# Six weight granules of the first projection multiplied in plain float32

## The reference, cut to what matters

```python
cond = silu(c)                                  # (1, 2048)
for layer in range(2):
    mod = cond @ ada_w[layer] + ada_b[layer]    # ada_w: 2048 x 6144 a layer
    shift, scale, gate = split(mod, 3)
    h = rms_norm(x, norm_w[layer]) * (1 + scale) + shift
    if layer == 0:                              # 16 heads of 128
        q, k, v, z = split(h @ w_in, 4)         # w_in: 2048 x 8192
        y = (attention(rope(norm(q)), rope(norm(k)), v) * silu(z)) @ w_out
    else:
        y = mlstm_branch(h, ...)                # w_in: 2048 x 16400, w_out: 4096 x 2048
    x = x + gate * y
```

## Time and profile before

| | us |
|---|---|
| median of 3 runs | 1509.64 |
| the profiled execution | 1510.05 |
| its span | 1508.2 |
| PE busy in the span | 1446.7 (96%) |
| DVE busy | 1105.2 (73%) |
| ACT busy | 744.6 (49%) |
| 16 DMA engines, hardware queue | 72.4% |
| HBM over the span | 239 GB/s |

### The profile page before, as it was taken

One profiled execution on the slowest core, in us unless ns is written; L12 is line 12 of the kernel. 1 busy time (PEld: TensorE's weight loads), 2 busy tenths in 40 slices (PEclk: granted clock), 3 DMA queues, 4 the chain that ended last, 5 costly groups with the idle time before them and its releaser, 6 DMA issues.

```text
span 1508.2 us, 19057 instructions
## 1 busy us (share of the span) xinstructions
PE 1446.7 (96%) x6679; PEld 1198.5 (79%) x6679; DVE 1105.2 (73%) x1234; ACT 744.6 (49%) x1002; POOL 45.3 (3%) x80
## 2 busy tenths in 40 slices
PE   2889999999999989999999999999999999999998
PEld 2767878888888867778888888888888888888886
DVE  5999898989898876878766566566566666656657
ACT  3544646454445455644544544544554454554452
POOL 1000010101000000010000000000000000000000
PEclk9999999999999999999999999999999999999999
DMA  9999889997989745798766566556566666566653
GB/s 337 387 392 387 272 282 323 322 342 275 332 296 353 269 125 182 241 324 300 251 184 187 175 190 186 173 189 189 173 194 181 172 191 193 167 189 190 178 182 112
DMA packets 198478, 361.47 MB, mean 240 GB/s; under 512 B 14240, under 2 KB 47352, under 8 KB 198412
## 3 DMA queue, kind: packets, MB, share of 16 engines
q1 hardware_dynamic: 198112, 359.60, 72.4%
q0 software_dynamic: 304, 1.06, 0.2%
HBM read 358.51 MB, written 2.11 MB: 239 GB/s over the span
## 4 chain that ended last, share of the span: by engine, by line
PE 84%; DVE 7%; issue 3%; ACT 3%; DMA 2%; SPq 1%; POOL 0%; DVEq 0%; ACTq 0%; POOLq 0%
PE proj L1331 24%; PE proj L1333 24%; PE proj L1332 24%; DVE ada_acc L852 3%; PE mix L1331 2%; PE mix L1332 2%; PE mix L1333 2%; DMA raw<-in_att_w_in 1%; DVE w_lo L833 1%; PE mix L1450 1%; DMA ada_more<-in_ada_w 1%; ACT w_hi L563 1%; PE mix L1517 1%; PE mix L1565 1%; PE mix L1484 1%
## 5 line engine op out<-in xcount | busy, mean ns | idle before, releaser
L833 DVE TENSOR_TENSOR w_lo<-raw,w_hi 128x1024 fp32r<-128x1024 f32 x480 | 585.4, 1221 | 355.1 <-ACT w_hi L563 354.3
L563 ACT ACTIVATE w_hi<-raw 128x1024 fp32r<-128x1024 f32 x480 | 507.7, 1061 | 681.2 <-PE proj L1333 578.6
L1331 PE MATMUL proj<-w_hi,h_hi 128*128 128x512 f32 x1472 | 583.2, 396 | 7.0 <-DVE h_lo L905 3.9
L1333 PE MATMUL proj<-w_hi,h_lo 128*128 128x512 f32 x1472 | 574.4, 390 | 0.0
L1332 PE MATMUL proj<-w_lo,h_hi 128*128 128x512 f32 x1472 | 574.0, 390 | 0.0
L1331 PEld LDWEIGHTS proj<-w_hi,h_hi 128*128 128x128 f32 x1472 | 277.0, 188 | 66.7 <-issue 9.0
L1333 PEld LDWEIGHTS proj<-w_hi,h_lo 128*128 128x128 f32 x1472 | 276.8, 188 | 58.6
L1332 PEld LDWEIGHTS proj<-w_lo,h_hi 128*128 128x128 f32 x1472 | 277.2, 188 | 57.5 <-issue 1.4
L852 DVE SCALAR_TENSOR_TENSOR ada_acc<-ada_raw,cond,ada_acc 128x1024 f32<-128x1024 f32 x148 | 188.8, 1276 | 2.8 <-DMA ada_raw<-in_ada_w 1.9
L1331 PE MATMUL proj<-w_hi,y_hi 128*128 128x512 f32 x320 | 125.9, 394 | 1.3 <-DVE stream L1003 1.3
L1333 PE MATMUL proj<-w_hi,y_lo 128*128 128x512 f32 x320 | 124.6, 389 | 0.0
(11 more groups left out here) (204 smaller groups left out, 940.3 us busy)
## 6 DMA issues: line engine op xcount, KB each, us to landing
raw<-in_mlstm_w_in SPq DMA_DIRECT2D x192, 512.0 KB, 3.7
ada_raw<-in_ada_w SPq DMA_DIRECT2D x160, 512.0 KB, 6.1
raw<-in_att_w_in SPq DMA_DIRECT2D x128, 512.0 KB, 7.1
raw<-in_mlstm_w_in SPq DMA_DIRECT2D x128, 256.0 KB, 3.0
raw<-in_mlstm_w_out SPq DMA_DIRECT2D x64, 512.0 KB, 4.3
raw<-in_att_w_out SPq DMA_DIRECT2D x32, 512.0 KB, 5.9
ada_more<-in_ada_w SPq DMA_DIRECT2D x16, 512.0 KB, 10.7
work<-in_ada_w SPq DMA_DIRECT2D x16, 512.0 KB, 10.3
```

The lines of the kernel that those rows point to most:

```text
L563: act.activation(w_hi[:, c % LEAD, :], raw[:, c % LEAD, :], ACT.Copy).then_inc(hi_ready, 1)
L833: dve.tensor_tensor(w_lo[:, c % LEAD, :], raw[:, c % LEAD, :], w_hi[:, c % LEAD, :].bitcast(F32), ALU.subtract).then_inc(lo_ready, 1)
L1331: pe.matmul(out_, a_hi, b_hi, start=start, stop=False, **kw)
L1333: return pe.matmul(out_, a_lo, b_hi, start=False, stop=stop, **kw)
```

## The change

`PLAIN` names the granules of v, group 0, places 0 to 5: 10, 11, 18, 23, 38 and 39. For these:

- PE multiplies the whole h (float32) with `raw` (float32), one plain float32 matmul for each K-tile and token tile, 4 instead of 12.
- `hi` and `lo` do no work on the weights: each copies one column of `cond` to a scratch column, and signals as before. `w_hi` and `w_lo` are not written.
- The last reader of `raw` is now PE, so SP's load of granule c+5 (15, 16, 23, 28, 43, 44) waits for `granule_used` of c, besides `lo_ready`.
- The whole h of layer 0 goes to `h_whole`, with a place of its own for each r, in place of two buffers taken in turn.

```diff
+PLAIN = [c for c in range(START) if ORDER0[c][:2] == (V_, 0) and ORDER0[c][2] < 6]
...
+        h_whole = part(0, 4096, "p (q n) -> p q n", q=UNIT)
+
+        def h_of(layer, q):
+            return h_full[:, q % 2] if layer else h_whole[:, q]
...
         def load0(sp, c):
 
+            if c - LEAD in PLAIN:
+                sp.wait_ge(granule_used, c - LEAD + 1)
             u, g, r = ORDER0[c]
...
         def hi(act, it, c):
 
+            if plain(it, c):
+                act.wait_ge(raw_in[c % LEAD], fills(it, c) * 16)
+                wait(act, granule_used, number(it, c) - LEAD + 1)
+                act.activation(passed[:, PLAIN.index(c):PLAIN.index(c) + 1], cond[:, 0:1], ACT.Copy).then_inc(hi_ready, 1)
+                return
...
         def lo(dve, it, c):
 
             dve.wait_ge(hi_ready, number(it, c) + 1)
+            if plain(it, c):
+                dve.tensor_copy(passed[:, PLAIN.index(c) + len(PLAIN):PLAIN.index(c) + len(PLAIN) + 1], cond[:, 0:1]).then_inc(lo_ready, 1)
+                return
...
             ps = pair0(u, g, r)
+            if c in PLAIN:
+                pe.wait_ge(raw_in[c % LEAD], fills(0, c) * 16)
+                for k in range(KG):
+                    for t in range(NT):
+                        op = pe.matmul(ps[:, t, :], h_whole[:, r, k * SEQ + t * P:k * SEQ + (t + 1) * P],
+                                       raw[:, c % LEAD, k * NC:(k + 1) * NC], start=r == 0 and k == 0, stop=False)
+                op.then_inc(granule_used, 1)
+                return
```

More of the change, by code:

```diff
@@ L159, in build @@
         cond = sb("cond", [P, KT])
+        passed = sb("passed", [P, 2 * len(PLAIN)])
         const = sb("const", [P, C_COS])
@@ L556, in sp_program, with plain @@
             sp.wait_ge(stored, 16 * CHUNKS)
+        def plain(it, c):
+            return isinstance(it, int) and it == 0 and c in PLAIN
         def hi(act, it, c):
+            if plain(it, c):
[3 more added lines that the diff above has]
+                return
             act.wait_ge(raw_in[c % LEAD], fills(it, c) * 16)
@@ L617, in h_make @@
                     continue
-                act.activation(h_full[:, q % 2, k * SEQ:(k + 1) * SEQ], src, ACT.Identity,
+                act.activation(h_of(layer, q)[:, k * SEQ:(k + 1) * SEQ], src, ACT.Identity,
                                scale=scale_c[:, layer, kt:kt + 1],
@@ L899, in h_rest @@
                         dve.wait_ge(h_act, KT + 2 * (q + 1))
-                    op = dve.tensor_scalar(h_full[:, q % 2, k * SEQ:(k + 1) * SEQ], src,
+                    op = dve.tensor_scalar(h_of(layer, q)[:, k * SEQ:(k + 1) * SEQ], src,
                                            scale_c[:, layer, kt:kt + 1], shift_c[:, layer, kt:kt + 1], ALU.mult, ALU.add)
@@ L904, in h_rest @@
             dve.wait_ge(h_act, KT * layer + 2 * (q + 1))
-            dve.tensor_tensor(h_lo[:, 2 * q:2 * q + 2, :].rearrange("p k t -> p (k t)"), h_full[:, q % 2, :],
+            dve.tensor_tensor(h_lo[:, 2 * q:2 * q + 2, :].rearrange("p k t -> p (k t)"), h_of(layer, q),
                               h_hi[:, 2 * q:2 * q + 2, :].rearrange("p k t -> p (k t)").bitcast(F32),
```

## The result

The changed kernel takes 1525.85 us (median of 4 runs, 1524.42 to 1526.94); the kernel before took 1509.75 beside it (1509.31 to 1510.75). The ratio is 1.0105, 95% interval [1.0093, 1.0117]: 16.1 us slower, where 8.3 were forecast. The profiled run took 1526.94 us, its span is 1525.1, 16.9 more than before.

What follows compares the result with a forecast made beforehand. PE was taken to bound the kernel (busy 96%), with DMA and DVE nearly full from 38 to 141 us; 0.5 + 2.5 + 1.6 + 1.4 + 2.3 = 8.3 us slower gave 1518 us, range 1512 to 1524.

Steps and rivals of the forecast that it cites:

- up to the end of granule 23: Opening, before load 28 leaves: only granule 16's late load counts, 0.5 us; granules 15 and 23 cost nothing.
- granules 38, 39: Where PE never waits: the longer plain products add 2 x 0.72 = 1.4 us.
- Product on PE: PE's plain granules: 4 float32 matmuls take 3.44 us against 2.72 for 12 float32r, 0.72 more each.
- Halves: ACT and DVE: replacements cost nothing; ACT's relief is worth nothing, DVE's counts only where data is there in time.
- The rival in which it wins: Opening: DVE sets the pace and is relieved of subtractions, 2.4 us faster, 1507; chance 5%.
- Granule 15: SP's load of granule 15, waiting for granule 10: still within the queue ahead of it, costs nothing.
- Granule 16: SP's load of granule 16, waiting for granule 11: 0.5 us reaches the `z_add` at 106.29, bounds 0 and 2.5.
- Granule 23: SP's load of granule 23, waiting for granule 18: lands at 109.1, before its high halves need it; costs nothing.
- Granule 28: SP's load of granule 28, waiting for granule 23: DMA runs dry, granule 29 2.5 us late, bounds 0 and 5.7.
- The clock behind granule 29: PE's granule 29, behind a 2.9 us wait: part at the lower clock, 1.6 us, bounds 0 and 2.72.
- Granules 43 and 44: SP's loads of these: the high half of 46 and the read of q come 2.3 us late, bounds 0 and 5.4.
- the loads come back slowly: Rival on the late loads: 6.85 us in place of 3.7 each, 15.7 us slower, 1525; chance 12%.

Runs made afterwards that it cites:

- the products alone: Six granules multiplied in plain float32, ACT and DVE still making both halves, no new SP waits, against the kernel before: 1512.38 us, ratio 1.0016.
- the products and the relief: The whole change with ACT's float32 copy of raw in place of SP's six waits, against the kernel before: 1510.89 us, ratio 1.0007.
- granule 10 alone: The change with PLAIN cut to granule 10 (wait ahead of load 15), against the kernel before: 1510.16 us, ratio 1.0002.
- granule 11 alone: The change with PLAIN cut to granule 11 (wait ahead of load 16), against the kernel before: 1512.91 us, ratio 1.0019.
- Alone, granule 18: The change with PLAIN cut to granule 18 (wait ahead of load 23), against the kernel before: 1514.91 us, ratio 1.0033.
- Granule 23 alone: The change with PLAIN cut to granule 23 (wait ahead of load 28), against the kernel before: 1519.25 us, ratio 1.0058.
- 10, 11 and 18: The change with PLAIN cut to these granules (waits ahead of loads 15, 16, 23), against the kernel before: 1513.08 us, ratio 1.0023.
- ada_w tiles ahead of load 28: The changed kernel with the three ada_w tiles behind loads 28, 29 and 30 put ahead of load 28: 1524.34 us, 1.0096 against the kernel before.
- granule 39 alone: The change with PLAIN cut to granule 39 (wait ahead of load 44), against the kernel before: 1515.66 us, ratio 1.0039.

## Why the prediction was wrong, point by point

The kind of loss was right, its size was not. Two steps failed: the "Nothing" for the late load of granule 23, and the 2.3 us for the loads of granules 43 and 44, priced by one tile's landing. They are 3.3 and 3.5 of the 8.6 us that are missing. The shift of the profiled run (16.9 us of span) divides so, beside the terms forecast:

| term | forecast | measured | read from |
|---|---|---|---|
| up to the end of granule 23 | 0.5 | 3.8 | load 28 leaves at 131.08, forecast 127.3 |
| load 28 to granule 29 | 2.5 | 3.6 | granule 29 is 7.4 late, less 3.8 |
| lower clock behind it | 1.6 | 2.3 | third sum 9.7 late (172.88 and 163.16), less 7.4 |
| granules 38, 39 | 1.4 | 1.4 | 6.88 us for both |
| loads 43 to 46 | 2.3 | 5.8 | 16.9 less 11.1 |
| sum | 8.3 | 16.9 | |

The forecast of 127.3 holds granule 23's own 0.7 us and not the 0.5. This is one trace's division. In others of kernels with all six waits the third sum is up to 12.6 us late, and the stretch from it to the fourth sum then costs less.

**Product on PE**: right, 3.44 us a granule. By the Trainium skill (FP8 and Floating Point Precision, section TensorE Precision Notes) four passes would have made it 4 x 0.907 = 3.63 (an estimate); the trace has 3.44.

**Halves**: what replaces them was counted as nothing, and DVE's relief only where tiles are there in time. The kernel with the products alone lost 2.6 us, and the one with the products and the relief 1.2. By this difference the relief was worth about 1.5 us where no load is late, within the noise of the two. No run has it beside the waits. The rival in which it wins was wrong, as its tiles did come late.

**Granule 15**: "Nothing" was right (0.6 for granule 10 alone).

**Granule 16**: 0.5 of bounds 0 to 2.5. With granule 11 alone it cost 3.2. In the profiled run of the change the load left at 83.6, granule 11 ran at the full clock, and granule 19 wasn't late. In the traces of the other kernels with the same wait it left at 84.5 to 87.9, and the first `z_add` started at 108.2 to 111.5.

**Granule 23: the first step that failed.** "Granule 24's high half only starts at 111.93, behind PE's granule 19. Nothing." I followed the weight tile to ACT, and forgot what I had written in the same part: every ada_w tile behind waits too. I had also counted three waits of PE in the opening and left out the 1.41 us ahead of the second sum, where these tiles are needed. Load 23 left 7.0 us late, and the last tiles of the second sum with it (DVE's step at 110.84 waits for its transfer). In the changed kernel the sum itself is only 0.6 us late (119.66 and 119.05). The rest comes by its wait of 3.61 us: behind it the sum takes 1.6 us more (3.54 and 1.92), and granule 22, mostly at the lower level, 1.5 more. These are the 3.8 us. Alone, granule 18 cost 5.3, which shows that its late load costs. That it costs by way of the clock is read from the traces. The kernel before has a stretch of the lower clock as well, from 109.1 to 112.6 us, but ahead of a wait of PE (1.41 us), which swallows it. In the change granule 19 runs at the full clock and PE comes to that wait 1.6 us earlier, so the wait is longer and the lower clock lies behind it, where load 28 hangs on granule 23.

**Granule 28**: right in mechanism. 4.0 us from issue to landing in place of 3.7, 8.8 us in place of 8.1 for six tiles. By the estimate from the 2.0 us of fixed cost that the Trainium skill gives (DMA: Bandwidth & Descriptors, section Anatomy of one DMA — SWDGE (gpsimd) path) it would have been 3.35, still further off. Granule 23 alone cost 9.5, where the two terms at granule 29 make 4.1; there granule 29 was 6.0 us late, and the lower clock behind it lasted nearly 6 us.

**The clock behind granule 29**: 2.3 of bounds 0 to 2.72. All of granule 29 ran at the lower level.

**Granules 43 and 44: the second step that failed.** 5.8 where I took 2.3, just over my bound of 5.4. The tile of granule 46 was 2.9 us later than reckoned, and I had looked no further than it. Up to ten microseconds pass without a transfer (2 and 3 GB/s from 170 to 180 us in the changed kernel), where the kernel before keeps its engines 0.75 and 0.95 busy. DVE gets its work late and has none of this time to give back: its first step with q stands at 201.39 instead of 185.03, 16.4 us late and 5.3 more than the terms above have made PE late, and the fourth sum on PE is 16.9 us late. In between PE waits for low halves, 1.30 us at 207.57 and 3.45 us at 219.42. Behind the second wait lies a stretch of the lower clock that I had not reckoned with either: the granule there takes 5.3 us, 2.5 more than at the full clock.

```profile
219.42 0.76 PE L1356 MATMUL proj<-w_hi,h_hi 128*128 128x512 f32 x1 [3.45 <-DVE w_lo L858]
```

One late load (granule 39's) is enough for such a loss.

Of the rivals, *the loads come back slowly* gave about the right time (15.7) by the wrong sums: its load 28 would have taken 6.85 us to land, and took 4.0.

## What to carry to other kernels

A wait added to a queue that issues in order must be priced for every transfer behind it, and to whom each goes. Count the time in which the DMA stands still and its readers go idle, and ask whether the stretch behind has the spare rate to make it up, in the transfers and in each engine that reads them: here DVE had none. By these traces a stretch of TensorE's lower clock costs little ahead of a wait of PE (109.1 to 112.6 us before) and 2.2 to 3.1 us behind a wait of more than 3 us, so a change that only moves a wait can cost. If a buffer's last reader moves from a fast engine to a late one, a copy on an idle engine (here ACT, 1.06 us a granule) can free it: 1.2 us lost instead of 16.1.

## What the runs showed of the hardware

- The same code came out with its lower clock in other places. Behind the first sum (78 to 88 us), kernels with the same instructions up to there showed the lower level for 0 (the change), 3.4 (10, 11 and 18) and 6.8 us (ada_w tiles ahead of load 28). The times of a kernel whose loads hang on PE spread more: 1509.97 to 1517.3 for granules 10, 11 and 18, against 1508.46 to 1511.47 for the kernel before beside it. That the one makes the other is likely and not shown.
- A transfer queue that has run dry took 4.0 us from the issue to the landing of its first tile of 512 KB (131.08 and 135.09), and was full soon: 387 GB/s in the third microsecond with transfers (134 to 135 us), and 404 in the kernel with granule 39 alone. There the rate then fell to between 205 and 348 GB/s from 178 to 184 us, before it stayed at 377 to 412 up to 190. What holds it back in those six microseconds was not tried.
